# Pair rows awaited by SP, latent tiles first, and the gate row applied to expert results in a two-layer hybrid backbone

## What is computed

```python
h = rmsnorm(x, norm1_w) * (1 + scale) + shift          # input norm
...
xl = xl + mod_l[5] * hier_moe(modulated_norm(xl, norm2_w, mod_l[3], mod_l[4]), p)
# in hier_moe, for each token: the sum over its two experts of
#   gate_w * ((silu(h @ w_gate) * (h @ w_up)) @ w_down)
...
return rmsnorm(xl, final_norm_w)
```

## Time and profile before

| | |
|---|---|
| median of 3 runs | 1458.87 us (1458.11 to 1460.78) |
| the profiled execution's own time | 1466.0 us |
| its span, first to last instruction | 1464.2 us |
| TensorE (PE) busy | 1211.7 us, 83% |
| VectorE (DVE) busy | 616.5 us, 42% |
| ScalarE (ACT) busy | 315.4 us, 22% |
| GpSimd (POOL) busy | 128.7 us, 9% |
| DMA | 322.18 MB, mean 220 GB/s |
| mean granted TensorE clock | 0.894 of full |

### The profile page before, as it was taken

The page is one execution under the profiler, slowest core; times in us unless marked ns, Lnnn a source line. Parts: engine busy times, 40 slices in busy tenths (PEclk is TensorE's granted clock), DMA queues, the critical chain, the costliest instruction groups (busy, mean ns, idle before and its releaser), DMA issues. The chain is left out here.

```text
span 1464.2 us, 19760 instructions
## 1 busy us (share of the span) xinstructions
PE 1211.7 (83%) x7632; PEld 799.1 (55%) x7632; DVE 616.5 (42%) x1223; ACT 315.4 (22%) x624; POOL 128.7 (9%) x144
## 2 busy tenths in 40 slices
PE   4899999989889669889887369999988498887880
PEld 1444547976669545545444156567767355544550
DVE  3434764036883542442222354844473522222223
ACT  3202012343443202131111122122522111111111
POOL 0000000000000012222221000000000122222210
PEclk8899999987889769999999779999869599999995
DMA  8733132325551638999999555343653469999982
GB/s 285 204 116 115 58 101 87 101 94 168 172 179 35 229 105 336 395 384 377 382 384 367 189 156 171 122 122 102 202 181 145 173 242 372 391 378 385 391 316 91
DMA packets 148149, 322.18 MB, mean 220 GB/s; under 512 B 28443, under 2 KB 111448, under 8 KB 123864
## 3 DMA queue, kind: packets, MB, share of 16 engines
q1 hardware_dynamic: 136664, 305.13, 57.8%
q0 software_dynamic: 11392, 15.77, 3.3%
HBM read 321.11 MB, written 21.23 MB: 234 GB/s over the span
## 5 line engine op out<-in xcount | busy, mean ns | idle before, releaser
L619 PE MATMUL bank<-hT,ring 128*128 128x512 f32 (+1 forms) x544 | 203.6, 531 | 1.7 <-DVEq L1219 1.0
L619 PE MATMUL bank<-ring,hT 128*128 128x256 f32 (+1 forms) x928 | 182.6, 352 | 1.5 <-DVE ysum L1640 1.5
L619 PE MATMUL bank<-ring,qkT 128*64 128x256 f32 x976 | 154.3, 417 | 33.5 <-DMA ring<-in_moe_w_up 25.6
L619 PEld LDWEIGHTS bank<-ring,hT 128*128 128x128 f32 x928 | 156.0, 195 | 21.2 <-issue 2.3
L1640 DVE TENSOR_TENSOR xbc<-xbc,bank 64x256 f32<-64x256 f32 x65 | 27.5, 423 | 308.8 <-ACT xbc L1301 260.5
L619 PEld LDWEIGHTS bank<-hT,ring 128*128 128x128 f32 x544 | 102.4, 190 | 97.6 <-issue 91.5
L619 PEld LDWEIGHTS bank<-ring,qkT 128*64 128x64 f32 x976 | 97.5, 150 | 64.2 <-issue 26.1
L619 PE MATMUL bank<-hT,qkT 128*64 128x256 f32 x496 | 89.3, 398 | 15.0 <-DMA xtok<-in_moe_w_up 7.8
L1234 POOL DMA_INDIRECT pair_rows<-hyT,zotok x65 | 60.0, 923 | 426.0 <-DVE xbc L1646 402.4
L1301 ACT ACTIVATE xbc<-bank 64x256 f32<-64x256 f32 x65 | 24.6, 378 | 291.8 <-PE bank L619 287.7
L619 PE MATMUL bank<-xtok,qkT 128*64 128x256 f32 x256 | 71.6, 443 | 13.2 <-DMA zotok<-in_moe_w_up 10.3
(11 more groups left out here) (322 smaller groups left out, 1689.0 us busy)
## 6 DMA issues: line engine op xcount, KB each, us to landing
ring<-in_w_mod SPq DMA_DIRECT2D x40, 1024.0 KB, 7.7
ring<-in_moe_w_down SPq DMA_DIRECT2D x31, 1024.0 KB, 12.4
ring<-in_moe_w_up SPq DMA_DIRECT2D x31, 1024.0 KB, 10.3
ring<-in_moe_w_gate SPq DMA_DIRECT2D x30, 1024.0 KB, 14.1
ring<-in_w_in SPq DMA_DIRECT2D x22, 1024.0 KB, 5.7
hT<-in_moe_w_gate SPq DMA_DIRECT2D x16, 1024.0 KB, 15.0
hT<-in_moe_w_up SPq DMA_DIRECT2D x15, 1024.0 KB, 10.0
hT<-in_moe_w_down SPq DMA_DIRECT2D x15, 1024.0 KB, 12.4
```

The source lines that it names most:

```text
L619: return nc.tensor.matmul(o, a, b, start=s, stop=e, **k)
```

## The change

- SP no longer waits for GpSimd's `pool_done` but for the last two scatters themselves. GpSimd's waits and drain move into the branch that is skipped.
- SP issues the first four weight loads of layer 2 before that wait; the generator `inproj_weights` allows it. The loop for surplus items uses other slots, 4 to 6.
- The pair tiles come in the order 2, 3, 0, 1, into other areas.
- In layer 2 the norm goes tile by tile. Tiles 2 and 3 go through first; TensorE transposes the latent half, ScalarE and VectorE evacuate four products each; both context tiles follow behind the first "hy" projection. `stage_end "norm1"` is gone, TensorE waits for the columns by name.
- In layer 2 VectorE scales both halves of an expert's result, by weight and gate row at once (`gated_halves`), and ScalarE none. `gate_rows(1)` of layer 2 moves from item 4 into the router. Layer 1 keeps its two halves and its gate product.
- At the end the gate product is gone and the two tiles go through norm and output one by one.

```diff
-        two_v = [a.rearrange("p (y d) -> p y d", y=2) for a in (big[:, 0:2048], big[:, 2048:4096],
-                                                              hT[:, 0:2048], hT[:, 2048:4096])]
+        two_v = [{t: a.rearrange("p (y d) -> p y d", y=2) for t, a in areas.items()} for areas in (
+            {2: hT[:, 0:2048], 3: hT[:, 2048:4096], 0: big[:, 0:2048], 1: qkT[:, 1024:3072]},
+            {2: big[:, 2048:4096], 3: hT[:, 0:2048]})]
...
         @block.sync
-                for who in ("pe", "act", "dve"):
-                    sp.wait_ge(*due(("end", who, l, "moe")))
+                if l + 1 < DEPTH:
+                    for _ in range(SLOTS):
+                        next(loading[l + 1])
                 with sp.If(flag != 0):
+                    for who in ("pe", "act", "dve"):
+                        sp.wait_ge(*due(("end", who, l, "moe")))
...
+                    sp.wait_ge(*due(("pairs written", l)))
-                for t in range(t0, NT):
-                    if t == t0:
-                        sp.wait_ge(*due(("pairs written", l)))
-                    sp.dma_start(two_v[t - t0], ...
+                for n in (1, 2):
+                    sp.wait_ge(*due(("scattered", l, EXPERTS + EXTRA[l] - n)))
+                for t, two in two_v[l].items():
+                    sp.dma_start(two, ...
...
         @block.tensor
+                    small_columns()
+                    for k in range(KB):
+                        input_columns(k, 1)
+                    pe.wait_ge(*due(("h1T", l, 1, "act")))
+                    pe.wait_ge(*due(("h1T", l, 1, "dve")))
...
                 for q in range(3):
                     channel_major("hy", 6, q, lambda blk: n0)
+                    if l and q == 0:
+                        for k in range(KB):
+                            input_columns(k, 0)
                 hyena_tokens(0)
+                if l:
+                    pe.wait_ge(*due(("h1T", l, 0)))
...
                 last.then_inc(pe_done, made(("rank", l)))
+                if l:
+                    gate_rows(1)
...
-                    if j == 4:
+                    if (l, j) == (0, 4):
                         gate_rows(1)
...
         @block.gpsimd
-                for u in range(2):
-                    pool.wait_ge(rows_out[u], tally.count[f"rows{u}_out"])
...
                 with pool.If(flag != 0):
+                    for u in range(2):
+                        pool.wait_ge(rows_out[u], tally.count[f"rows{u}_out"])
...
-                pool.drain().then_inc(pool_done, tick("pool_done", ("pairs written", l)))
+                    pool.drain().then_inc(pool_done[l], tick(f"pool{l}_done", ("pairs written", l)))
...
         @block.scalar
+                    input_squares(2)
+                    input_squares(3)
+                    input_roots(2, 1)
+                    input_roots(3, 1)
+                    act.wait_ge(*due(("ab", l, 0)))
+                    for k in range(0, KB, 2):
+                        input_columns(k, 1, ("h1T", l, 1, "act"))
+                    input_squares(0)
+                    input_squares(1)
+                    input_roots(0, 1)
+                    input_roots(1, 1)
...
-                    if j:
+                    if l == 0 and j:
                         left_half(j - 1)
...
         @block.vector
+                    for t in (2, 3):
+                        pair_sum(l - 1, t)
+                        pair_gate(l - 1, t)
+                        pair_add(l - 1, t)
+                    inverse(l, 2, 1)
+                    pair_sum(l - 1, 0)
+                    dve.wait_ge(*due(("rstd", l, 1, 2)))
+                    normed_input(2)
+                    inverse(l, 3, 1)
+                    pair_gate(l - 1, 0)
+                    dve.wait_ge(*due(("rstd", l, 1, 3)))
+                    normed_input(3)
+                    dve.wait_ge(*due((f"nw{l}_in",)))
+                    modulators(0)
+                    pair_add(l - 1, 0)
+                    for k in range(1, KB, 2):
+                        input_columns(k, ("h1T", l, 1, "dve"))
+                    pair_sum(l - 1, 1)
+                    pair_gate(l - 1, 1)
+                    pair_add(l - 1, 1)
+                    inverse(l, 0, 1)
+                    dve.wait_ge(*due(("rstd", l, 1, 0)))
+                    normed_input(0)
...
                     conv("hy", blk, hy_v, 20, 38, 6, t0 // 2, *([("hy z", l, 0)] if blk == 1 else []))
+                    if l and blk == 0:
+                        inverse(l, 1, 1)
+                        dve.wait_ge(*due(("rstd", l, 1, 1)))
+                        normed_input(1)
...
+                def gated_halves(j):
+                    if j >= 2:
+                        dve.wait_ge(*due(("scattered", l, j - 2)))
+                    name = ("down", l, j)
+                    dve.wait_ge(*due(("made", name)))
...
+                    for half in range(2):
+                        r_ = slice(R2 * half, R2 * half + R2)
...
+                        stt(res_v[0:R2, j % 2, 512 * half:512 * half + 512], bank(name)[r_, :], weight_of[r_, j:j + 1],
+                            grow_v[r_, 1, 512 * half:512 * half + 512], MUL, MUL, *names)
...
+            pair_sum(DEPTH - 1, 2)
+            pair_add(DEPTH - 1, 2)
+            pair_sum(DEPTH - 1, 3)
+            inverse(DEPTH, 2, 1)
+            pair_add(DEPTH - 1, 3)
             dve.wait_ge(*due(("norm_in",)))
+            normed_output(2)
+            inverse(DEPTH, 3, 1)
+            normed_output(3)
```

More of the change, by code:

```diff
@@ L488, in _ @@
                     first_single(7)
[L489 to L504, removed]
+                for _ in loading[l]:
+                    pass
                 wgt, wup = (A[name][l].rearrange("g e (p k) f -> (g e) p (k f)", k=KB) for name in ("moe_w_gate", "moe_w_up"))
@@ L723, in small_columns, with input_columns @@
                     nc.tensor.transpose(b[:, 0:78], prow[0:78, :], ident[0:78, 0:78]).then_inc(pe_done, made(("pcol", l)))
-                if l:
-                    small_columns()
-                for k in range(KB):
-                    for s in range(2):
-                        b = product(("h1", l, k, s))
-                        pe.wait_ge(*due(("xn", l, 1)))
-                        for t in range(2):
-                            last = nc.tensor.transpose(b[:, t * P:(t + 1) * P], xn_v[:, 2 * s + t, k::KB], ident[:, :])
-                        last.then_inc(pe_done, made(("h1", l, k, s)))
+                def input_columns(k, s):
+                    b = product(("h1", l, k, s))
+                    pe.wait_ge(*due(("xn", l, 1, 2 * s + 1)))
+                    for t in range(2):
+                        last = nc.tensor.transpose(b[:, t * P:(t + 1) * P], xn_v[:, 2 * s + t, k::KB], ident[:, :])
+                    last.then_inc(pe_done, made(("h1", l, k, s)))
                 if l == 0:
+                    for k in range(KB):
+                        for s in range(2):
+                            input_columns(k, s)
                     filter_step(l, 5, (4,))
@@ L1269, in _ @@
                         flag = pool.value_load(more_flag[0:1, :], min_val=0, max_val=MORE_ITEMS)
-                    pool.wait_ge(*due(("result", l, j, "act")))
+                    if l == 0:
+                        pool.wait_ge(*due(("result", l, j, "act")))
                     pool.wait_ge(*due(("result", l, j, "dve")))
@@ new lines, in input_columns @@
+                def input_columns(k, s, *names):
+                    act.wait_ge(*due(("made", ("h1", l, k, s))))
+                    b, o = bank(("h1", l, k, s)), hT_v[:, k, s * L:(s + 1) * L]
+                    fn(o, b[:, 0:L], ACT.Identity, ("read", ("h1", l, k, s)), *names,
+                       scale=ab_v[:, 0, k, 1 - s:2 - s], bias=ab_v[:, 1, k, 1 - s:2 - s])
+                if l == 0:
+                    act.wait_ge(*due(("x_in",)))
+                    for t in range(NT):
+                        input_squares(t)
+                    mod_rows(l, 2)
+                    mod_rows(l, 3)
+                    filter_step(l, 3)
+                    input_roots(0, NT)
@@ L1391, in _ @@
                     part_after()
+                    if l and q == 0:
+                        for k in range(KB):
+                            input_columns(k, 0, ("h1T", l, 0))
                 filter_input(0)
```

194 lines of the change are left out of this document (105 added, 89 removed).

## The result

The changed kernel takes 1440.6 us (median of 4 runs, 1436.7 to 1445.0) against 1458.5 (4 runs, 1458.1 to 1460.8): ratio 0.987, 95% interval 0.985 to 0.989, 17.9 us by the medians. Run again beside later experiments it took 1438.6 (6 runs, 1437.3 to 1445.3): ratio 0.9876 (0.9847 to 0.9905).

What follows compares the result with a forecast made beforehand. It took the kernel as bound by full DMA in the expert stages, with a serial chain in the hole behind each. Gains of 8.3 + 1.9 + 9.3 = 19.5 us took 1458.9 to 1439.4, rounded 1439; range 1433 to 1447.

Steps and rivals of the forecast that it cites:

- Part 1: Pair rows of layer 1: reads issued at 826.65 despite the weight prefetch, first tile used at 831.55; gain 1.6 us.
- Part 2: Latent tiles first at layer 2's start: transposes 7.9 us sooner, half of them before the projection 2.7, 3.9 coming back.
- transition: First hole, between the layers: 1.6 + 7.9 + 2.7 - 3.9 = 8.3 us gained.
- Part 3: Gate row out of item 4 of layer 2, where it delays the load stream: gain 1.9 us, ends 0 and 2.0.
- Part 4: Layer 2's end: gated halves on VectorE lose 1.6 us, SP's own wait gains 5.8, tile by tile gains 5.1.
- tail: Last item to output: -1.6 + 5.8 + 5.1 = 9.3 us gained.
- The rival of a scatter that hardly suffers: Layer 1's last scatter lands in 4 us instead of 7 despite the prefetch: 3 us more, 1436; chance 0.18.
- What comes back: Start of layer 2: tile 1 stall 0.5, context transposes 2.65, clock 0.7; 3.9 us lost, ends 2.7 and 7.
- the second rival: First hole gives little: later reads, low clock through the projection (3), late tile 1; transition 2, time 1446; chance 0.15.
- Slower by VectorE: VectorE's result halves pace layer 2's experts; at 6.6 us each, 25 us lost against 19.5 gained, 1464; chance 0.02.
- The branch as a new wait: At the tail SP's branch or two waits take as long as GpSimd's drain: 5.8 missing, 1445; chance 0.05.
- The signs: Right if reads at 825 to 828, transposes 9 to 10 us earlier, second projection near 860.7; wrong if reads at 823.

Runs made afterwards that it cites:

- its second trace: The changed kernel run once more as it is, on the same chip as three later edits: 1438.6 us (6 runs).

## Why the prediction was right, point by point

Forecast 1439, measured 1440.6 and 1438.6. The terms, from the trace of the changed kernel (in brackets its second trace):

| step | predicted | measured |
|---|---|---|
| Part 1, reads behind the scatter | 7.06 us | 6.22 (6.31) |
| Part 1, gain up to the first use | 1.6 | 2.0 (2.0) |
| Part 2, first use to transposes | 7.9 | 8.0 (8.0) |
| Part 2, half of the transposes | 2.7 | 2.9 (2.9) |
| Part 2, back | 3.9 | 4.4 (4.3) |
| transition | 8.3 | 8.55 (8.66) |
| Part 3, gate row | 1.9 | 1.9, in place |
| Part 4, halves on VectorE | -1.6 | -1.5 |
| Part 4, clock in the last down product | none | -1.0 (none) |
| Part 4, SP's own wait | 5.8 | 5.9 (5.9) |
| Part 4, tile by tile | 5.1 | 4.9 (5.05) |
| tail | 9.3 | 8.2 (9.6) |

- **The prefetch** delays the scatter, as the step said, by 3.8 us; 7.0 from the loaded stage was 0.7 too long. But the first use doesn't hang on the scatter as the step had it: the tile's read stands behind the four megabytes and lands 2.54 us after them, so that it is used 5.33 after its issue, not 4.93. The rival of a scatter that hardly suffers falls: landing by 4 us didn't occur with the loads ahead. Nor would it have brought its 3 us, for the same reason. That the term came out near (2.0 for 1.6) is in part luck. The Trainium skill ("DMA: Bandwidth & Descriptors", Queues, rings and completion order) says that a DMA engine alternates between its queues packet by packet. The 5.9 to 6.3 us, shorter than any of rows 6, fit that in direction, but no run here varied the weights' row length, so it isn't shown.
- **What comes back** was right in sum by errors that met, which is luck. The clock's term (0.7) was mis-sized: it took 2.5, since the clock rose 9.5 us after the first transpose and not 5 to 6. For that reason TensorE came late enough that the predicted stall for tile 1 (0.5) didn't show. In the kernels whose clock rose in time the stall is there, 1.17 to 1.18. The context transposes took 1.9 instead of 2.65, and 2.1 in those kernels: sixteen in a row are shorter than four times the four of the earlier trace rows. The upper end of this term was mis-sized as well: the projection spent 5.1 us at the low clock and lost 2.5 by it, so half clock through all of it would cost some 7 by estimate, not the 3.5 of the step and the 3 of the second rival.
- **Part 3** holds in its place only: the row's 1.9 us are gone there, but no run shows them in the whole time, and the later scatter and gather of Part 4 take some of it back at the same item.
- **Slower by VectorE**: 1.53 us for both halves, hidden while the loads run; it shows in the last item and at item 4. The branch as a new wait: reads 2.5 us behind the scatter, so no.
- Of 23.9 us between the two spans, 2.5 lay ahead of the change, and 2.7 in stretches of layer 2 that it leaves as they are, 2.1 of them from item 4's load to the last Silu. I don't count those as its work: summed by the table with its gate row, it is 18.7 (20.2), and the medians say 17.9 and, against 1457.0, 18.3.
- **The signs**, with the scatter's 2.5 us taken out: reads at 825.8 (823.34 in the trace itself, next to the sign of being wrong), first transposes 10.0 earlier, second projection at 860.5; DMA share 1.00 from 1250 to 1400. The clock was low through half of the first projection, not all of it.

## What to carry to other kernels

A wait for another engine's end of stage can hold a drain that nobody needs; wait for the transfers themselves. Loads issued ahead of such a wait aren't free, even into free slots with nothing to collide on the engines: the transfer that is waited for shares the DMA engines with them, and 4 MB ahead made a 2.4 us scatter 6.2. The reads behind it then landed only after all 4 MB. Where a change shortens a chain, mark the trace by that chain's own first event: here the spans of two executions differed by 5 us more than the change had won.

## What the hardware showed beside

- The rise of the clock goes with the spacing of the work ahead, and not evenly. In six traces TensorE had been idle for 24.06 to 24.18 us ahead of the 16 transposes, and the first projection took 9.21 to 9.65 us. In five others with 5.15, 19.93, 19.96, 29.60 and 32.33 us of idle time it took 7.14 or 7.15, and so it did before the change with 34.09. An idle time that is shorter isn't better by itself. These executions differ in more than the idle time, so what sets the rise isn't shown.
- Behind an idle time of 1.76 or 1.77 us ahead of the last down product the clock stayed up in eight traces and fell during the product in one.
- The table load took 1.28 us, and the root followed it 0.02 later. It ran on ScalarE beside VectorE's add of the second tile, so little of it lay on the path.
